# Two layer changes reordered over three engines, and a bias matmul in the rounded format

## The reference

```python
x = _layernorm(ALPHA * x + y, ln_w[layer], ln_b[layer])        # layers 0 and 1
# mLSTM: dmat[t,s] = bcum[t] - bcum[s] + log_i[s]; m_t is its running maximum
s_qk = einsum('bhtd,bhsd->bhts', qx, kx) * exp(dmat - m_t[..., None])
# forgetting attention
s = einsum('bhqd,bhkd->bhqk', q, k) * scale + F[..., None] - F[..., None, :]
```

## Time and profile before

| | |
|---|---|
| median of 3 runs | 1917.11 us (1912.95 to 1918.15) |
| the profiled execution | 1915.61 us |
| its span, first to last instruction | 1913.9 us |
| mean granted TensorE clock | 0.995 |
| TensorE matmul / VectorE / ScalarE busy | 98% / 65% / 51% |
| DMA | 319.28 MB, mean 167 GB/s |

### The profile page before, as it was taken

The page is one execution under the profiler, slowest core; times in us unless marked ns, Lnnn a source line. Parts: engine busy times, 40 slices in busy tenths (PEclk is TensorE's granted clock), DMA queues, the critical chain, the costliest instruction groups (busy, mean ns, idle before and its releaser), DMA issues.

```text
span 1913.9 us, 25132 instructions
## 1 busy us (share of the span) xinstructions
PE 1868.4 (98%) x9089; PEld 1567.5 (82%) x9089; DVE 1248.7 (65%) x1689; ACT 980.8 (51%) x1508; POOL 28.2 (1%) x107
## 2 busy tenths in 40 slices
PE   8999989999999999997999999999999999999999
PEld 6888878778888888886888888888878888878787
DVE  5566666587556746667777778777866555566664
ACT  4455564355465545535545454544435545566652
POOL 4000000000000000000000000000000000000000
PEclk9999999999999999998999999999999999999999
DMA  6665444478789877564545454444456666545453
GB/s 231 206 187 154 138 122 144 141 208 189 176 151 212 177 175 173 198 213 124 172 140 158 145 184 142 152 155 154 144 167 198 187 189 184 154 150 155 138 165 118
DMA packets 170206, 319.28 MB, mean 167 GB/s; under 512 B 16600, under 2 KB 20848, under 8 KB 169344
## 3 DMA queue, kind: packets, MB, share of 16 engines
q1 hardware_dynamic: 168992, 313.70, 56.7%
q10 hardware_dynamic: 576, 4.19, 0.5%
q0 software_dynamic: 544, 0.13, 0.0%
HBM read 315.88 MB, written 2.10 MB: 166 GB/s over the span
## 4 chain that ended last, share of the span: by engine, by line
PE 45%; DVE 2%; ACT 2%; issue 2%; ACTq 0%; DVEq 0%
PE acc L286 13%; PE acc L288 13%; PE acc L287 13%; PE ps L2541 3%; PE ps L515 1%; ACT whi L248 1%; DVE wlo L256 1%; PE ps L2525 0%; DVE arena L1936 0%; PE ps L380 0%; ACT arena L1398 0%; ACT arena L1334 0%; PE ps L2515 0%; PE ps L548 0%; PE ps L2622 0%
## 5 line engine op out<-in xcount | busy, mean ns | idle before, releaser
L256 DVE TENSOR_TENSOR wlo<-wraw,whi 128x1024 fp32r<-128x1024 f32 (+3 forms) x616 | 713.9, 1178 | 417.1 <-ACT whi L248 414.5
L248 ACT ACTIVATE whi<-wraw 128x1024 fp32r<-128x1024 f32 (+3 forms) x616 | 614.8, 1017 | 346.7 <-PE acc L288 340.0
L286 PE MATMUL acc<-whi,ta_hi 128*128 128x512 f32 x1664 | 662.3, 398 | 13.1 <-DVE wlo L256 10.7
L288 PE MATMUL acc<-whi,ta_lo 128*128 128x512 f32 x1664 | 650.8, 391 | 0.0
L287 PE MATMUL acc<-wlo,ta_hi 128*128 128x512 f32 x1664 | 649.7, 390 | 0.0
L286 PEld LDWEIGHTS acc<-whi,ta_hi 128*128 128x128 f32 x1664 | 313.9, 189 | 79.5 <-issue 12.7
L288 PEld LDWEIGHTS acc<-whi,ta_lo 128*128 128x128 f32 x1664 | 313.5, 188 | 67.0
L287 PEld LDWEIGHTS acc<-wlo,ta_hi 128*128 128x128 f32 x1664 | 314.2, 189 | 62.2
L286 PE MATMUL acc<-whi,tb_hi 128*128 128x512 f32 (+1 forms) x704 | 279.1, 396 | 8.2 <-DVE wlo L256 6.5
L288 PE MATMUL acc<-whi,tb_lo 128*128 128x512 f32 (+1 forms) x704 | 271.4, 386 | 0.0
L287 PE MATMUL acc<-wlo,tb_hi 128*128 128x512 f32 (+1 forms) x704 | 270.8, 385 | 0.0
(11 more groups left out here) (302 smaller groups left out, 1339.5 us busy)
## 6 DMA issues: line engine op xcount, KB each, us to landing
wraw<-in_ml_w_in SPq DMA_DIRECT2D x128, 512.0 KB, 5.8
wraw<-in_a_w_in SPq DMA_DIRECT2D x128, 512.0 KB, 4.0
wraw<-in_kv_w SPq DMA_DIRECT2D x64, 512.0 KB, 4.0
wraw<-in_b_w_in SPq DMA_DIRECT2D x64, 512.0 KB, 4.4
wraw<-in_mla_w_in SPq DMA_DIRECT2D x48, 512.0 KB, 4.8
wraw<-in_mla_w_out SPq DMA_DIRECT2D x32, 512.0 KB, 3.8
wraw<-in_ml_w_out SPq DMA_DIRECT2D x32, 512.0 KB, 4.6
wraw<-in_a_w_out SPq DMA_DIRECT2D x32, 512.0 KB, 4.4
```

What stands on the lines that cost most here:

```text
L248: nc.scalar.activation(whi[:, n % SPLIT, :, 0:w], wraw[:, n % RAW, :, 0:w], ACT.Copy).then_inc(w_high, 1)
L256: nc.vector.tensor_tensor(wlo[:, n % SPLIT, :, 0:w], wraw[:, n % RAW, :, 0:w], whi[:, n % SPLIT, :, 0:w].bitcast(F32), ALU.subtract).then_ ...
L286: nc.tensor.matmul(o, xh, wh, start=first, stop=False)
L288: m = nc.tensor.matmul(o, xl, wh, start=False, stop=end)
```

## The change

- **First change.** In quarters 0 and 2 weight and bias are applied to the stream itself, before the turn, by two fused VectorE instructions (`ln_weigh`: minus the mean, times weight; `ln_offset`: times the root, plus bias); ScalarE and VectorE then split the turned PSUM bank directly. Quarters 1 and 3 get weight and bias from ScalarE, none from VectorE, each with a `tmpT` buffer of its own. `ln_stream` has four quarters left and runs at units 4 to 8 of `l1_0`.
- **Second change.** `ln_scale` in pieces of one and three quarters; VectorE weighs only quarter 1, ScalarE 0, 2 and 3; other orders on all engines; `ln_stream` at units 6 to 14, the first evacuation of `l2` at unit 15 instead of 14.
- **Bias.** `split_rows` writes a cleared 128x256 tile in the rounded format, the rounded rows in rows 0 to n and what rounding left off in rows 32 to 32+n. `pick` has ones at c and 32+c of column c, so one rounded matmul adds both. `negM` and `negR` use a k-tile of `TBf` and `TA` that is free at that time.

```diff
-            nc.scalar.activation(ta_bank(0, b, q), t.rearrange("p (k t) -> p k t", t=P), ACT.Copy).then_inc(tr_hi, 1)
+        def by_rows(n, q):
+            return n == 0 and q % 2 == 0
+        def ln_slot(n, q):
+            return tmpT[:, q // 2 if n == 0 else q % 2, :]
+        def ln_slot_free(eng, n, c):
+            eng.wait_ge(tr_lo, c - 3 if n == 0 else c - 1)
+        def ln_turned(n, c, q):
+            t = ps[:, c % 4, :] if by_rows(n, q) else ln_slot(n, q)
+            return t.rearrange("p (k t) -> p k t", t=P)
...
-                    (ident[:, c:c + 1].to_broadcast([P, P]), ones[:, 0:n])]
+                    (pick[:, c:c + 1].to_broadcast([P, P]), negR[:, 0:n])]
...
 # ScalarE, first change
+            c = turn.n
             ln_rstd(0, 0)
-            ln_hi(act, own, turn, 0, 0, 0)
             step(act, high, evac, "l1_gates", 0)
             step(act, high, evac, "l1_gates", 1)
-            ln_hi(act, own, turn, 0, 0, 1)
-            ln_hi(act, own, turn, 0, 0, 2)
+            ln_hi(act, own, turn, 0, c, 0, 0)
+            ln_affine_act(act, own, 0, c + 1, 1)
+            ln_hi(act, own, turn, 0, c + 1, 0, 1)
+            ln_hi(act, own, turn, 0, c + 2, 0, 2)
             ln_rstd(0, 1)
-            ln_hi(act, own, turn, 0, 0, 3)
+            ln_affine_act(act, own, 0, c + 3, 3)
+            ln_hi(act, own, turn, 0, c + 3, 0, 3)
             step(act, high, evac, "l1_gates", 2)
             step(act, high, evac, "l1_gates", 3)
-            for q in range(4):
-                ln_hi(act, own, turn, 0, 1, q)
-            for p in range(SPLIT, length("l1_gates")):
-                step(act, high, evac, "l1_gates", p)
+            ln_hi(act, own, turn, 0, c + 4, 1, 0)
+            ln_affine_act(act, own, 0, c + 5, 1)
+            ln_hi(act, own, turn, 0, c + 5, 1, 1)
+            step(act, high, evac, "l1_gates", 4)
+            ln_hi(act, own, turn, 0, c + 6, 1, 2)
+            ln_affine_act(act, own, 0, c + 7, 3)
+            step(act, high, evac, "l1_gates", 5)
+            step(act, high, evac, "l1_gates", 6)
+            ln_hi(act, own, turn, 0, c + 7, 1, 3)
+            step(act, high, evac, "l1_gates", 7)
...
 # ScalarE, second change (after)
+            ln_rstd(1, 0)
+            step(act, high, evac, "l2", 0)
+            step(act, high, evac, "l2", 1)
+            ln_affine_act(act, own, 1, c, 0)
+            ln_hi(act, own, turn, 1, c, 0, 0)
+            ln_hi(act, own, turn, 1, c + 1, 0, 1)
+            ln_affine_act(act, own, 1, c + 2, 2)
+            ln_hi(act, own, turn, 1, c + 2, 0, 2)
+            ln_rstd(1, 1)
+            step(act, high, evac, "l2", 2)
+            ln_affine_act(act, own, 1, c + 3, 3)
+            ln_hi(act, own, turn, 1, c + 3, 0, 3)
+            ln_affine_act(act, own, 1, c + 4, 0)
+            ln_hi(act, own, turn, 1, c + 4, 1, 0)
+            step(act, high, evac, "l2", 3)
+            ln_affine_act(act, own, 1, c + 6, 2)
+            ln_hi(act, own, turn, 1, c + 5, 1, 1)
+            ln_hi(act, own, turn, 1, c + 6, 1, 2)
+            step(act, high, evac, "l2", 4)
+            ln_affine_act(act, own, 1, c + 7, 3)
+            ln_hi(act, own, turn, 1, c + 7, 1, 3)
...
 # VectorE, first change (after)
+            ln_stats(0, "l0_out", 0)
+            ln_weigh(0, 0)
+            ln_offset(0, 0)
+            ln_scale(0, 0, 1, 2)
+            ln_scale(0, 0, 3, 4)
+            step(dve, low, evac, "l1_gates", 0)
+            step(dve, low, evac, "l1_gates", 1)
+            ln_weigh(0, 2)
+            ln_offset(0, 2)
+            ln_lo(dve, turn, 0, c, 0, 0)
+            ln_stats(0, "l0_out", 1)
+            ln_lo(dve, turn, 0, c + 1, 0, 1)
+            ln_weigh(1, 0)
+            ln_lo(dve, turn, 0, c + 2, 0, 2)
+            ln_offset(1, 0)
+            ln_scale(0, 1, 1, 2)
+            ln_lo(dve, turn, 0, c + 3, 0, 3)
+            ln_weigh(1, 2)
+            ln_lo(dve, turn, 0, c + 4, 1, 0)
+            ln_offset(1, 2)
+            ln_scale(0, 1, 3, 4)
+            step(dve, low, evac, "l1_gates", 2)
+            step(dve, low, evac, "l1_gates", 3)
+            ln_lo(dve, turn, 0, c + 5, 1, 1)
+            ln_lo(dve, turn, 0, c + 6, 1, 2)
+            step(dve, low, evac, "l1_gates", 4)
+            step(dve, low, evac, "l1_gates", 5)
+            step(dve, low, evac, "l1_gates", 6)
+            ln_lo(dve, turn, 0, c + 7, 1, 3)
+            step(dve, low, evac, "l1_gates", 7)
...
 # VectorE, gates_b
-                dve.wait_ge(l1["pads"], 2)
-                nc.vector.tensor_scalar(negM[0:8, :], grow[:, 4, :], -1.0, None, ALU.mult).then_inc(l1["g_m"], 1)
                 nc.vector.tensor_tensor(grow[:, 5, :], grow[:, 2, :], grow[:, 4, :], ALU.add).then_inc(l1["g_m"], 1)
+                own.then(nc.vector.tensor_scalar(grow[:, 4, :], grow[:, 4, :], -1.0, None, ALU.mult))
+                split_rows(negM, grow[:, 4, :], 8, l1["g_m"])
+
+            def split_rows(dst, src, n, done):
+                own.then(nc.vector.tensor_scalar(dst, ones[:, 0:T], 0.0, None, ALU.mult))
+                own.then(nc.vector.tensor_copy(dst[0:n, :], src))
+                nc.vector.tensor_tensor(dst[32:32 + n, :], src, dst[0:n, :].bitcast(F32), ALU.subtract).then_inc(done, 1)
...
 # VectorE, second change (after)
+            ln_stats(1, "l1_out", 0)
+            ln_scale(1, 0, 0, 1)
+            ln_scale(1, 0, 1, 4)
             step(dve, low, evac, "l2", 0)
+            ln_affine_dve(dve, turn, 1, c + 1, 1)
+            ln_lo(dve, turn, 1, c, 0, 0)
+            ln_stats(1, "l1_out", 1)
+            ln_lo(dve, turn, 1, c + 1, 0, 1)
+            ln_lo(dve, turn, 1, c + 2, 0, 2)
+            ln_scale(1, 1, 0, 1)
             step(dve, low, evac, "l2", 1)
             step(dve, low, evac, "l2", 2)
+            ln_scale(1, 1, 1, 4)
+            ln_lo(dve, turn, 1, c + 3, 0, 3)
+            ln_lo(dve, turn, 1, c + 4, 1, 0)
+            ln_affine_dve(dve, turn, 1, c + 5, 1)
             step(dve, low, evac, "l2", 3)
+            ln_lo(dve, turn, 1, c + 5, 1, 1)
+            ln_lo(dve, turn, 1, c + 6, 1, 2)
+            step(dve, low, evac, "l2", 4)
+            ln_lo(dve, turn, 1, c + 7, 1, 3)
...
 # TensorE (after)
+            XN = (((1, 2, 4, 3), (5, 6, 7, 8)), ((9, 10, 10, 10), (11, 12, 12, 12)))
+            for i in range(SPLIT):
+                last_products_of("l0_out", out0_src, 0, i)
+            for i in range(3):
+                last_products_of("l0_out", out0_src, 1, i)
+            ln_turn(0, 0, 0)
+            ln_turn(0, 0, 1)
+            last_products_of("l0_out", out0_src, 1, 3)
+            ln_turn(0, 0, 2)
+            ln_turn(0, 0, 3)
+            ln_turn(0, 1, 0)
+            ln_turn(0, 1, 1)
...
                 products(pe, "l1_gates", p, in_src)
+                if p == 0:
+                    ln_turn(0, 1, 2)
+                    ln_turn(0, 1, 3)
...
+            last_products_of("l1_out", out1_src, 1, 0)
+            last_products_of("l1_out", out1_src, 1, 1)
+            for q in range(3):
+                ln_turn(1, 0, q)
+            last_products_of("l1_out", out1_src, 1, 2)
+            last_products_of("l1_out", out1_src, 1, 3)
             pe.wait_ge(tr_lo, at + 1)
             products(pe, "l2", 0, in_src, 0, (0,))
             ln_turn(1, 0, 3)
+            ln_turn(1, 1, 0)
             products(pe, "l2", 1, in_src, 0, (0,))
             pe.wait_ge(tr_lo, at + 2)
             products(pe, "l2", 2, in_src, 0, (0,))
+            for q in range(1, 4):
+                ln_turn(1, 1, q)
             pe.wait_ge(tr_lo, at + 5)
             products(pe, "l2", 0, in_src, 0, (1,))
             products(pe, "l2", 1, in_src, 0, (1,))
+            products(pe, "l2", 3, in_src, 0, (0,))
...
 # VectorE, beside l3_q unit 6
+            def bias_rows():
+                tile_done(dve, "l3_kv", 1, 3)
+                dve.wait_ge(l3["f_ok"], 2)
+                split_rows(negR, negF, 16, l3["f_ok"])
```

More of the change, by code:

```diff
@@ L419, in ta_bank, with ln_affine_act, ln_hi, ln_affine_dve @@
             return TA[hl][:, 4 * q:4 * q + 4, b * P:(b + 1) * P]
[L421 to L433 removed]
+        def by_rows(n, q):
[7 more added lines that the diff above has]
+            return t.rearrange("p (k t) -> p k t", t=P)
+        def ln_affine_act(act, own, n, c, q):
+            act.wait_ge(tr_pe, c + 1)
+            ln_slot_free(act, n, c)
+            t = ln_slot(n, q)
+            for j in range(4):
+                w, s = ln_cols(n, q, j)
+                own.mark(nc.scalar.activation(t[:, j * P:(j + 1) * P], ps[:, c % 4, j * P:(j + 1) * P],
+                                              ACT.Identity, bias=s, scale=w))
+        def ln_hi(act, own, cnt, n, c, b, q):
+            if by_rows(n, q):
+                act.wait_ge(tr_pe, c + 1)
+            elif n == 1 and q == 1:
                 act.wait_ge(tr_tmp, cnt.w + 1)
                 cnt.w += 1
[L436 removed]
+            else:
+                own.sync()
+            nc.scalar.activation(ta_bank(0, b, q), ln_turned(n, c, q), ACT.Copy).then_inc(tr_hi, 1)
```

(47 more changed lines are left out.)

104 lines of the change are left out of this document (22 added, 82 removed).

## The result

The changed kernel takes 1892.09 us (median of 4 runs, 1890.58 to 1893.14), the kernel before 1915.36 (4 runs): ratio 0.9877, 95% interval 0.9860 to 0.9895. The forecast was 1893 from 1917.11, so 24.1 less; the medians differ by 23.3, and the ratio of 0.9877 stands for 23.6. The profiled execution of the changed kernel took 1891.89 with a span of 1890.1.

A forecast was written before the change was run, and what follows sets the result against it. TensorE, holding matmuls for 98% of the span, was taken to bound the kernel. Terms 2.9 + 11.7 + 9.3 = 23.9 us off the profiled 1915.61 gave 1891.7, so a median of 1893; range 1889 to 1902.

The forecast's parts named there:

- term of 2.9: First layer change: the new orders start `l1_0` 2.9 us earlier; bounds 1.5 and 3.9.
- walk of the new order: First layer change, stepped through in its new order from the residual at 371.55: `l1_0` starts at 393.9.
- walk of the old order: First layer change, same method tested on the old order: `l1_0` reached at 396.7 against 396.26 seen.
- upper bound of 3.9: First layer change: largest gain allowed, 3.9 us, from the walk at full clock.
- bound of 1.0: Split of unit 9, queued behind the longer gate chain on VectorE: costed at 0, at most 1.0 us.
- term was 11.7: Second layer change: new orders gain 11.7 us, with one 4 us stretch at half clock; bounds 8.0 and 13.4.
- upper bound of 13.4: Second layer change: unit 7 of `l2` ends 13.4 us earlier with the clock full all the way.
- Rival (b): Second layer change keeps the low clock, waits only change places: gain 5 us, time 1900; chance 0.14.
- (e): Both layer changes: edits do not act, chain not order holds them, only the bias gain comes: 1908; chance 0.04.
- 9.3 forecast: Bias matmuls in rounded format: 6.8 us less in the attention, 2.5 in the mLSTM; bounds 5.5 and 10.5.
- Rival (d): Attention groups: VectorE and ScalarE bound them, so the bias change gives nothing there, 6.8 us less gain, 1900; chance 0.07.
- (a) to (d): Forecast within bounds 0.61, second change's low clock kept 0.14, weight-load waits 0.07, attention bound by VectorE and ScalarE 0.07; stated sum 0.90.

## Why the prediction was right

**First change.** 2.4 us in the trace for a term of 2.9. The residual of block 1 came 6.57 us after the first (379.79), 6.75 by the walk; the wait in front of its turns is 3.58. The walk of the new order ended at 22.35 (393.9 - 371.55) and the trace has 22.34. The miss is the walk of the old order, 0.4 late, which was taken as the other end of the difference (396.7 - 393.9). That the new walk met the trace to 0.01 is partly luck: a fused weigh or offset takes 0.74 to 0.75, not 0.69, and was made up for elsewhere. The upper bound of 3.9, the new order at full clock, was too low: against the kernel before that is 24.71 - 20.20 = 4.5, and 4.2 (24.42 - 20.20) with the clock full in both.

**The gate chain.** It grew by the expected amount and stayed covered: VectorE began it earlier, since the late pass was over, and neither `gates_c` nor unit 9 has a wait. The run with the bias part alone shows that this was the reason: with the old late pass TensorE waits 0.69 us at unit 9, inside the bound of 1.0.

**Second change.** The waits were forecast as 2.1 and 0.8 and came as 1.60 and 0.47, unit 4 after 23.30 us where 23.5 to 25.5 was the range named. The term was 11.7 with one stretch of half clock; in this execution there was none, and the gain is 12.35 to unit 4 plus 1.4 of low clock after it, 13.8 (47.94 to 34.18 in the table), just above the upper bound of 13.4 that had the clock full all the way. Two of the other four profiles with the same orders and this wait unfilled have the drop (0.79 in the window 862 to 870 us), and the two half units behind the wait then take 4.4 us instead of 2.84: one stretch costs 1.6, about as the term had it (1.7, from 13.4 to 11.7), but comes only sometimes. With it the gain is 12.2 (47.94 to 35.75). The size of the term also rests on the one profile of before, whose 47.94 stands between 45.54 and 49.38. Rival (b), that waits only change places and term 2 is 5, is out, and so is (e).

**The bias.** 9.3 forecast. The trace gives 8 x 0.86 = 6.9 in the attention and 2.4 in the mLSTM's stretch; alone it measured 9.2 by its ratio. A head was priced at 0.11 + 0.31 and gives 0.16 for the 128 columns (1635.34 to 1635.78 against 1618.40 to 1618.68) and the other 0.26 to 0.27 for the 256, so by these starts the sum was right and the two prices in it were not. Rival (d) is out: the wait once a group is still 1.6 us, and the whole saving of two pairs shows between two of them. Small slips of the prediction, without weight for the result: the attention's products sum to 6.7, not 6.8; the prices stated for 128 columns would give bounds of 7.4 and 10.1, not 5.5 and 10.5; the chances of (a) to (d) sum to 0.89; and a score pair of 2.6 us is 2.43 in the rows read to the next projection matmul. The Trainium skill (TensorE: Matmul & The Clock Gate, Part 3, what overlaps and what doesn't) has a weight load hidden only where the row group differs; by the estimate made from that, 0.11 us more for each of 32, a second copy of the bias would have cost 7 us. It cost 3.3 by the medians and 3.5 by the traces: the trace disagrees, and the measurement decides.

**What nearly cancelled.** The start of the changed kernel's profile is 1.67 us later than before, 1.6 of it for a reason that has nothing to do with the edits: a drop of the clock at 240 us. Against it stands the second change's gain of 13.8 for a term of 11.7. Both are the clock's, and the forecast of 1893 owes part of its 0.9 us to that: that the sum came so near is luck, while the three terms came within 0.5, 2.1 and 0.1 us of what was measured.

## What to carry to other kernels

A wait of TensorE costs what it takes and, where TensorE's own work sets the length of the stretch behind it, the low clock that may follow; where other engines set that length, the low clock is nearly free. So filler matmuls gave 2.1 us in the new order of the first change and 0.3 in the old. After a reordering look again at which engine sets the length of the stretch: dummy matmuls in the wait (1888.85 us, the fastest complete version here) may have become worth it. A small operand that is split once into rounded upper and lower parts and stacked along the contraction turns each plain matmul with it into one rounded one, here 0.43 us less for a pair of one with 128 and one with 256 columns, and the changes of format around it cost nothing that the runs show.
